# A hybrid decoder layer with 32 experts: one product for all bias lines, paired score products, and a shorter hand-over at the end

## The reference

```python
h = modulate(rms_norm(x, norm_mix), shift, scale)        # shift, scale from silu(c) @ w_ada + b_ada
q, k, v, u = split(h @ w_in)                             # 512, 128, 128, 512 columns
s = einsum(q, k) * 64**-0.5 + rel_table[t5_bucket(rel)]  # 8 heads, 2 kv heads, window of 128
s = where((rel >= 0) & (rel < 128), s, -1e30)            # softmax with one sink per head, times v
x = x + gate_mix * (concat([attn, pool]) @ w_out)        # pool: multi-scale mixer of u
h = modulate(rms_norm(x, norm_ffn), shift_ffn, scale_ffn)
y = moe_ffn(h)                                           # 32 experts, top 4, clamped SwiGLU
x = x + gate_ffn * y                                     # for the prompt rows and the sample rows
```

## Time and profile before

| | us |
|---|---|
| median of 3 runs | 1351.2 |
| profiled execution | 1354.14 |
| its span, first to last instruction | 1352.6 |
| TensorE busy | 1218.1 (90%) |
| VectorE busy | 713.6 (53%) |
| ScalarE busy | 489.6 (36%) |
| GpSimd busy | 326.7 (24%) |
| moved by DMA | 474.16 MB, mean 351 GB/s |

### The profile page before, as it was taken

How to read it: one execution, slowest core, us unless ns; L and a number is a source line. 1 busy time by engine, 2 the same in 40 slices (tenths; PEclk the granted TensorE clock), 3 DMA queues, 4 the chain that set the end, 5 groups by cost and what they waited for, 6 DMA issues and landing times.

```text
span 1352.6 us, 17632 instructions
## 1 busy us (share of the span) xinstructions
PE 1218.1 (90%) x6408; PEld 725.9 (54%) x6408; DVE 713.6 (53%) x1118; ACT 489.6 (36%) x703; POOL 326.7 (24%) x353
## 2 busy tenths in 40 slices
PE   5899799969999979998899889998889998999973
PEld 2455455553675735755675247555457555565531
DVE  3532663463785874553794234546534536667530
ACT  5111432231564633332573133333323333546320
POOL 2232221031222213113322311143321133232111
PEclk9899799979999989999899999998979998999976
DMA  9950786489999999999999999999999999999993
GB/s 332 345 127 5 263 302 215 158 316 385 400 391 363 406 408 393 404 385 371 402 414 407 398 397 407 388 363 402 403 393 408 359 345 408 413 407 412 403 413 113
DMA packets 101404, 474.16 MB, mean 351 GB/s; under 512 B 17417, under 2 KB 19896, under 8 KB 55162
## 3 DMA queue, kind: packets, MB, share of 16 engines
q1 hardware_dynamic: 82282, 444.76, 82.2%
q0 software_dynamic: 18384, 26.53, 8.0%
q10 hardware_dynamic: 650, 1.72, 0.4%
HBM read 459.47 MB, written 32.66 MB: 364 GB/s over the span
## 4 chain that ended last, share of the span: by engine, by line
PE 53%; DMA 12%; DVE 6%; issue 4%; ACT 1%; POOL 1%; SPq 0%; POOLq 0%; DVEq 0%; ACTq 0%
PE bank L2422 51%; DMA raw<-in_w 5%; DVE rawr L2242 2%; DMA out_y_prompt<-gu,slot_tok 2%; DMA yd<-gu,idx_s 2%; DMA yd<-ost,idx_s 2%; PE bank L2470 1%; PE bank L2446 1%; ACT hi L2059 1%; POOL gu L1932 1%; DVE gu L2206 1%; DVE gu L2204 0%; DVE ost L2276 0%; ACT ost L2042 0%; SPq L553 0%
## 5 line engine op out<-in xcount | busy, mean ns | idle before, releaser
L2242 DVE TENSOR_TENSOR rawr<-raw,hi 128x1024 fp32r<-128x1024 f32 x288 | 351.6, 1263 | 106.3 <-ACT hi L2059 104.8
L2059 ACT CAST hi<-raw 128x1024 fp32r<-128x1024 f32 x288 | 294.8, 1048 | 166.1 <-PE bank L2422 140.9
L2422 PE MATMUL bank<-raw,xT_even 128*64 128x512 f32 (+1 forms) x704 | 135.2, 600 | 0.1
L1918 POOL DMA_INDIRECT yd<-ost,idx_s x31 | 56.5, 1824 | 325.4 <-ACT ost L2042 324.5
L2422 PE MATMUL bank<-raw,aT 128*32 128x256 f32 (+1 forms) x992 | 113.7, 478 | 11.5 <-DMA raw<-in_w 11.5
L2422 PE MATMUL bank<-raw,xT_odd 128*32 128x512 f32 (+1 forms) x544 | 84.8, 647 | 15.8 <-DMA raw<-in_w 15.8
L2422 PE MATMUL bank<-hi,xTh_odd 128*128 128x512 f32 x224 | 76.8, 426 | 19.8 <-DVE rawr L2242 19.5
L2422 PE MATMUL bank<-hi,aTh 128*128 128x512 f32 x240 | 77.3, 404 | 12.5 <-DVE rawr L2242 12.5
L2422 PE MATMUL bank<-hi,xTh_even 128*128 128x512 f32 x256 | 84.5, 412 | 3.9 <-DVE rawr L2242 3.8
L2204 DVE TENSOR_SCALAR gu<-bank 128x512 f32<-128x512 f32 (+1 forms) x50 | 31.4, 627 | 103.2 <-PE bank L2422 103.2
L2024 ACT ACTIVATE gu<-gu 128x512 f32<-128x512 f32 (+1 forms) x50 | 29.2, 583 | 145.6 <-DVE gu L2204 145.6
(11 more groups left out here) (387 smaller groups left out, 1847.6 us busy)
## 6 DMA issues: line engine op xcount, KB each, us to landing
raw<-in_w SPq DMA_DIRECT2D x356, 1024.0 KB, 14.7
raw<-in_w SPq DMA_DIRECT2D x48, 512.0 KB, 13.1
raw<-in_w_ada SPq DMA_DIRECT2D x21, 1024.0 KB, 7.7
w_in_sb<-in_w_in SPq DMA_DIRECT2D x4, 1280.0 KB, 16.2
w_out_sb<-in_w_out SPq DMA_DIRECT2D x4, 1024.0 KB, 9.0
early<-in_w SPq DMA_DIRECT2D x4, 1024.0 KB, 12.4
ada_more<-in_w_ada SPq DMA_DIRECT2D x3, 1024.0 KB, 13.8
xs<-in_x_prompt SPq DMA_DIRECT2D x4, 512.0 KB, 14.1
```

The source lines that it names most:

```text
L1918: gp.indirect_dma_start(yd_of[n], bass.IndirectOffsetOnAxis(ap=m.idx_s[:, p % 6, b:b + 1], axis=0), out_rows(p, b), None, bounds_check=lim ...
L2059: nc.scalar.copy(m.hi[:, (2 * n + h) % HI, :], m.raw[:, slot, h * D:(h + 1) * D]).then_inc(hi_done, 1)
L2242: v.tensor_tensor(m.rawr[slot][:, half], m.raw[:, slot, half], m.hi[:, (2 * n + h) % HI, :].bitcast(F32), ALU.subtract).then_inc(lo_done, 1)
L2422: return nc.tensor.matmul(out, lhsT, rhs, start=start, stop=stop, skip_group_check=True)
```

## The change

1. `relrep` holds each head's 33 numbers once, as 8 columns. One product gives all 8 lines in rows 0 to 7 of bank 6, one copy takes them to `line` (now 8 partitions), and the transfer to `skew` reads each of the 8 lines 128 times.
2. `score` goes by pairs of banks: for each of the two products of a bank, first the even then the odd j; the waits of both banks stand ahead.
3. VectorE scales the rows of pass 30 (`NE - 2`) ahead of its wait for `gf_in`, not behind it.
4. SyncE waits for `samp_done` itself; GpSimd neither waits for it ahead of its loop nor raises `summed`. In the body for an extra pass, which doesn't run here, a wait for `samp_done` is added.

```diff
-        m.relrep = at("relrep", [NE + 1, NH, P], F32, raw0 + 6 * SLOT_B)
+        m.relrep = at("relrep", [NE + 1, NH], F32, raw0 + 6 * SLOT_B)
-        m.line = at("line", [P, NH, LINE], F32, raw0 + 4 * SLOT_B)
+        m.line = at("line", [NH, LINE], F32, raw0 + 4 * SLOT_B)
...
-            gp.wait_ge(s.line_ready, NH)
-            gp.dma_start(m.skew.rearrange("h (p n) -> p h n", n=LINE), m.line[:]).then_inc(s.skew_out, 16)
+            gp.wait_ge(s.line_ready, 1)
+            gp.dma_start(m.skew.rearrange("h (p n) -> h p n", n=LINE),
+                         m.line[:].unsqueeze(1).to_broadcast([NH, P, LINE])).then_inc(s.skew_out, 16)
...
-            v.tensor_copy(m.relrep[:], m.relb[:].unsqueeze(2).to_broadcast([NE + 1, NH, P])).then_inc(s.rel_ready, 1)
+            v.tensor_copy(m.relrep[:], m.relb[:]).then_inc(s.rel_ready, 1)
...
-                if k % 2:
-                    for h in (k - 1, k):
-                        v.wait_ge(s.line_tr, h + 1)
-                        v.tensor_copy(m.line[:, h, :], bank[6 + h % 2][:, 0:LINE]).then_inc(s.line_ready, 1)
+                if k == 1:
+                    v.wait_ge(s.line_tr, 1)
+                    v.tensor_copy(m.line[:], bank[6][0:NH, 0:LINE]).then_inc(s.line_ready, 1)
...
-            def bias_line(h):
-                if h >= 2:
-                    pe.wait_ge(s.line_ready, h - 1)
-                mm(bank[6 + h % 2][:, 0:LINE], m.relrep[:, h, :], m.oh_line[:, 0:LINE], start=True,
-                   stop=True).then_inc(s.line_tr, 1)
+            def bias_lines():
+                mm(bank[6][0:NH, 0:LINE], m.relrep[:], m.oh_line[:, 0:LINE], start=True, stop=True).then_inc(s.line_tr, 1)
...
-                        if not k % 2:
-                            bias_line(k)
-                            bias_line(k + 1)
+                        if not k:
+                            bias_lines()
...
-                for j in banks:
...
-                    for a in range(2):
-                        last = mm(bank[4 + j][:, a * 256 + c0:a * 256 + 256], m.qT[half, 2 * g + a, tok(t)],
-                                  m.kT[half, g, t * P - P + c0:t * P + P], start=True, stop=True)
-                    last.then_inc(s.sc_ready, 1)
+                for g in range(2):
+                    pair = [j for j in banks if j // 2 == g]
+                    for j in pair:
...
+                    for a in range(2):
+                        for j in pair:
+                            half = slice(64 * (j % 2), 64 * (j % 2) + 64)
+                            last = mm(bank[4 + j][:, a * 256 + c0:a * 256 + 256], m.qT[half, 2 * g + a, tok(t)],
+                                      m.kT[half, g, t * P - P + c0:t * P + P], start=True, stop=True)
+                            if a:
+                                last.then_inc(s.sc_ready, 1)
...
-            sp.wait_ge(unit_used, extra * UNITS + ALL_USED)
-            sp.wait_ge(summed, 1)
+            sp.wait_ge(samp_done, extra * 16 + 16 * BB[NE])
+            sp.sem_inc(summed, 1)
...
-            gp.wait_ge(samp_done, 16 * BB[NE])
             gp.wait_ge(extra_ready, 1)
             extra = extras(gp, one)
-            gp.sem_inc(summed, 1)
...
+            scale_rows(NE - 2)
             v.wait_ge(gf_in, 16 * 6)
-            scale_rows(NE - 2)
```

More of the change, by code:

```diff
@@ L1435, in _ @@
                 if t == 1:
-                    pe.wait_ge(s.line_ready, NH)
+                    pe.wait_ge(s.line_ready, 1)
                     mm(bank[6][0:64, 0:P + 1], m.rel64[:].rearrange("p b h -> p (b h)"), m.oh_s[:], start=True,
@@ L1491, in score @@
                 pe.wait_ge(s.kT_ready, t + 1)
-                for j in banks:
[L1493 to L1502, removed]
-                    for a in range(2):
-                        last = mm(bank[4 + j][:, a * 256 + c0:a * 256 + 256], m.qT[half, 2 * g + a, tok(t)],
-                                  m.kT[half, g, t * P - P + c0:t * P + P], start=True, stop=True)
-                    last.then_inc(s.sc_ready, 1)
+                for g in range(2):
+                    pair = [j for j in banks if j // 2 == g]
+                    for j in pair:
+                        if t:
+                            pe.wait_ge(s.sc_used, 4 * (t - 1) + j + 1)
+                        else:
+                            pe.wait_ge(s.U_ready, j + 1)
+                        if not j and t >= 2:
+                            pe.wait_ge(s.pm_done, t - 1)
+                        if j == 3 and t >= 2:
+                            pe.wait_ge(s.mr_ready, 2 * t + 2)
+                    for a in range(2):
+                        for j in pair:
[4 more added lines that the diff above has]
+                                last.then_inc(s.sc_ready, 1)
             def turn_P(t, j):
@@ L1981, in one @@
                 gp.wait_ge(far_ready, x + (NE + 1))
+                gp.wait_ge(samp_done, x * 16 + 16 * BB[NE])
                 gp.sem_inc(stores, 1)
```

## The result

The changed kernel took 1335.63 us, the median of 3 runs (1335.62 to 1337.6), against 1351.2 before; the ratio is 0.9887 with a 95% interval of 0.9864 to 0.991. The forecast was 1339.6. Six more runs of the same kernel later gave 1337.05 (1333.27 to 1339.95) against 1352.12 of before on that chip, a ratio of 0.9892 [0.9867, 0.9918]. The profiled execution has a span of 1334.0 us and a granted clock of 0.951, against 1352.6 and 0.945.

The account below looks back on a forecast made before the run. Bounds: TensorE in the projections, the DMA weight stream in the expert passes, a chain of small waits at the end. Head 5.8 plus end 5.8 made 11.6, taken from the median 1351.2: 1339.6 us, range 1335.5 to 1345.5.

Parts of the forecast that it names:

- Head: TensorE's projections: one bias product instead of eight, start 0.5 earlier at 41.1, tile 0 ends 5.3 to 6.0 earlier, 5.8 taken.
- the two prices: Cost of one projection step at full clock: 1.39 us by the first tile's cycles, 1.30 by the second tile.
- What is late next: Behind the shorter projection: tile 0's query rows ready at 66.5, TensorE needs them at 67.0; at worst half a microsecond lost.
- Skew transfer: Same 1,532 KB from 8 partitions: 23 us taken, bounds 11.6 and 71, no cost unless it takes 44 us.
- a rival of 0.03: Slow skew transfer holds the sample rows and TensorE behind the u products from 44 us on; at worst 1367; chance 0.03.
- Pairing: Score products by pairs of banks: 0.2 and 0.4 us for tiles 0 and 1, off the path; cost 0, bounded by ±0.6.
- End: Last 15.6 us: earlier scaling and SyncE's own wait let the sums be read at 1341.8, 5.8 us earlier.
- its signs: Things to look for in the profile after, among them expert stage's first weight load and last TensorE product 5 to 6 earlier.
- the spells of lower clock fall better: Rival: six microseconds less at the lower clock level give 3 us back, 1336.6; chance 0.06.
- the first rival: Head's gain is lost before the weight stream, only the end is left: 1345.4; one of the two gains lost, chance 0.13.
- nothing there runs by the wall clock: Argument against the first rival: between 130 and 300 transfers are gated by what TensorE and DVE have used.
- as long as its bytes, whenever it starts: Expert passes, 303 to 1300: a weight stream at DMA share 1.00 and 395 GB/s, its length independent of its start.

Follow-up runs that it names:

- e8_twice: The changed kernel with the skew transfer done twice, one behind the other, its waiters now waiting for the second: 1374.97 us, ratio 1.0192.
- e7_rows: The changed kernel with each line kept in 16 partition rows, so that the skew transfer reads 128 partitions: 1337.87 us, ratio 0.9909.
- e2_pairs: The kernel before with only the score products by pairs of banks: 1353.02 us, ratio 1.0005.
- e5_nopairs: The changed kernel without the pairing, the score order staying bank by bank: 1336.23 us, ratio 0.9898.
- e4_scale: The kernel before with only pass 30 scaled ahead of the wait for g_last, SyncE still waiting for GpSimd: 1347.96 us, ratio 0.998.
- the four sister versions: Head and end changed as in the changed kernel: e5_nopairs, e7_rows, e7_rows with 18 filler products (1337.78 us), the changed kernel with 8 (1338.43 us).

## Why the prediction was right

- **Head, 5.8 forecast, 5.56 measured** (5.65 by all profiles). The start moved by 0.18, not 0.5; the copy did shrink (0.15 us for 33x8), but two profiles of the same head differ by more than this at the start, so what became of the half microsecond isn't shown. A step was 1.29, the lower of the two prices (1.30), as taken. The clock rose at about 48.4 (a mean of 0.76 over 14.63 us is 7.0 us at the lower level), not at 47.7. The tile ended at 56.05, 0.25 behind the 55.8 of the forecast.
- **What is late next.** Nothing was. ScalarE's cast started at 55.76, one earlier than assumed, the last kd copy at 65.23 against 66.5 forecast, and TensorE came at 67.28: 1.8 us of cover, not 0.5.
- **Skew transfer, cost 0.** Right in cost and in the chain that sets the threshold (e8_twice), wrong in the size: 23 us taken, 40.3 measured, 39 GB/s. It lies inside the bounds of 11.6 and 71, but what was called a rival of 0.03 was missed by 4 us. That the cost came out at nothing with a term so far off is luck in part. The Trainium skill (SBUF — State Buffer, "Door 1: The DMA port swizzle") led to an estimate of 29 us, over a quarter short of the 40.3 measured. Its direction agrees (e7_rows: 17.5 from 128 partitions), but e7_rows also reads each partition less often.
- **Pairing, cost 0.** Right: e2_pairs and e5_nopairs. The 0.4 forecast for tile 1 is of the order of what was seen (0.23) and lost in the wait ahead. The Trainium skill (TensorEngine Tiling (Array Packing), "Key Properties") is not gainsaid: products of the two halves overlapped before too, so there was little to pair.
- **End, 5.8 forecast, 5.83 measured,** with SyncE's loop as the last to arrive, as the working had it. For edit 3 without edit 4 the prediction said "some 4"; e4_scale shows 3.0. The other single case, edit 4 alone, priced at 3.8, wasn't tried.
- **Sum and the rest.** 11.6 forecast; 11.4 by the traces' two pieces and 11.9 by the runs at equal clock. So the terms of the sum were right. The measured change is larger, 15.6 by the first medians and 15.1 by the second, and that the first median, 1335.63, still lies in the range, whose lower bound is 1335.5, is luck. The 4.0 by which it lies under the forecast goes with the clock: its three runs had 0.949 to 0.952, in the mean 5.4 thousandths over before's, and 5.4 x 0.70 is 3.8. ScalarE's rows of the last pass, and with them TensorE's last product, came 12.8 us earlier (1323.95, before 1336.73), not 5 to 6 as the prediction had it among its signs.
- **Where its reasoning failed.** The rival "the spells of lower clock fall better", held at 0.06 and 3 us, is no other outcome but comes on top of the sum. Its size was near (3 us, where 3.1 to 4.0 came on top), its chance far too small. The sentence against the first rival, "nothing there runs by the wall clock", doesn't hold: the work at 135 moved by 5.6, while the last stretch of the lower level before 160 moved by 13.0 (150.1 to 137.1) and shrank from 13.7 us to 3.4. And the expert stage is not quite "as long as its bytes, whenever it starts": it varied by 4.6 us between profiles. What stays open is why the changed kernel's mean clock is higher by 0.0039 +- 0.002: the missing long stretch accounts for it in the profiles, but unprofiled runs show no stretches, and the four sister versions, at 0.9470 in the mean, have less than half of it.

## What to carry to other kernels

Where the granted clock differs between the runs of two kernels, give the change both plainly and at equal clock (here 14.7 and 11.9), and take one profile each for the pieces alone: it can hold or miss a 13.7-us stretch at the lower level, worth 6.8 us at the end of the attention stage, of which another execution of the same kernel kept little (4.6 us at 303, 0.9 at the end). When a filler or any other edit is to test a pause, look first whether the pause was there in that very execution. When a repeated store is cut down to fewer source partitions, ask how much slack its chain has, and measure the landing, since here 40.3 of 44 us were used. At a kernel's end, let the engine that reads wait for the data itself, not for an engine that has other work to finish.

## What the runs showed of the hardware

- A transfer of 1,532 KB takes 40.3 us from 8 partitions, each read 128 times (39 GB/s), 17.5 from 128 partitions, each read 8 times, and 11.6 in the layout before.
- In seven profiles a pause of TensorE of 2.9 to 4.6 us went with 6.8 to 13.7 us at 1.2 GHz from its last microseconds on; in three a pause of 1.8 to 1.95 us, and in three a pause filled with small products, did not. In before's profile the clock stayed at the lower level through 12.66 us of unbroken products.
- Score products of the two halves of the array cost the same bank by bank and by pairs: twelve records of the third tile take 1.96 us by pairs (after) and 1.96 in plain order (e5_nopairs), of the fourth 1.99 in both. Six products one behind another would be 2.6, so they overlap in either order.
